# Attention of layer 1: who copies the turned weights out of PSUM

## What is computed

```python
s_loc = jnp.einsum('bnqgrd,bnkgd->bngrqk', qb, kband) * scale      # band of 3 blocks of 128
s_ctx = jnp.einsum('bnqgrd,bkgd->bngrqk', qb, ck) * scale          # 128 cached keys
s_loc = jnp.where(valid, s_loc, MASK_VALUE)
m = jnp.maximum(jnp.max(s, -1), sink)                              # s = both parts in one row
e = jnp.exp(s - m)
p = e / (jnp.sum(e, -1) + jnp.exp(sink - m))
o = p[..., :nk] @ vband + p[..., nk:] @ cv
```

## Time and profile before

| | us |
|---|---|
| median of 3 runs | 2339.85 |
| lowest, highest run | 2335.29, 2341.19 |
| the profiled execution, its own time | 2339.42 |
| its span, first to last instruction | 2337.6 |
| TensorE busy | 2101.0 (90%) |
| VectorE, ScalarE, GpSimd busy | 1437.2, 1266.3, 751.5 |
| mean granted TensorE clock | 0.957 |

### The profile page before, as it was taken

The page is one execution under the profiler, slowest core; times in us unless marked ns, Lnnn a source line. Parts: engine busy times, 40 slices in busy tenths (PEclk is TensorE's granted clock), DMA queues, the critical chain, the costliest instruction groups (busy, mean ns, idle before and its releaser), DMA issues.

```text
span 2337.6 us, 53990 instructions
## 1 busy us (share of the span) xinstructions
PE 2101.0 (90%) x22874; PEld 1285.3 (55%) x22874; DVE 1437.2 (61%) x1779; ACT 1266.3 (54%) x1651; POOL 751.5 (32%) x546
## 2 busy tenths in 40 slices
PE   4999787978989999999899879878879999999994
PEld 3666456845565555555667557645544444444441
DVE  3362656668362121215558667585379999999975
ACT  3534554556444242424543765465378777777762
POOL 0332115433404242424223236432123333333332
PEclk9999898989999999999999989989979999999997
DMA  9442690020312222224231000100367788991124
GB/s 290 138 145 94 217 289 30 4 59 4 93 37 92 71 90 72 86 75 143 90 119 39 1 11 4 45 18 23 131 230 226 240 272 280 321 344 54 32 91 166
DMA packets 246503, 278.45 MB, mean 119 GB/s; under 512 B 61345, under 2 KB 221965, under 8 KB 246159
## 3 DMA queue, kind: packets, MB, share of 16 engines
q1 hardware_dynamic: 237056, 251.99, 34.4%
q0 software_dynamic: 6128, 21.50, 2.5%
q10 hardware_dynamic: 3103, 1.85, 0.3%
HBM read 359.97 MB, written 29.11 MB: 166 GB/s over the span
## 4 chain that ended last, share of the span: by engine, by line
PE 75%; DVE 9%; ACT 8%; issue 3%; DMA 2%; POOL 1%; SPq 1%; DVEq 0%; ACTq 0%; POOLq 0%
PE ps L2307 74%; DVE arena L1674 1%; ACT mix L1460 1%; DVE arena L1678 1%; DVE mix L1674 1%; DMA wbuf<-in_w_mod 1%; DVE small L1902 1%; SPq L726 1%; PE ps L3074 1%; ACT arena L1170 1%; DVE hT L1674 1%; ACT hT L1466 1%; POOL extra L915 1%; ACT arena L1051 1%; DVE const L1674 1%
## 5 line engine op out<-in xcount | busy, mean ns | idle before, releaser
L2307 PE MATMUL ps<-hT,mix 128*128 128x512 f16 (+2 forms) x3024 | 378.1, 287 | 22.7 <-DVE hT L1674 10.4
L2307 PE MATMUL ps<-w,xgT 128*128 128x512 f16 x1632 | 365.6, 381 | 3.6 <-ACT xgT L1571 3.6
L2307 PEld LDWEIGHTS ps<-hT,mix 128*128 128x128 f16 x3024 | 227.4, 99 | 171.1 <-issue 20.7
L2220 DVE SCALAR_TENSOR_TENSOR w<-wst,w 128x2048 f16<-128x2048 f32 x136 | 312.2, 2334 | 5.9 <-ACT w L1557 5.9
L1035 POOL TENSOR_TENSOR a<-aval,a 128x256 f16<-128x256 f32 x68 | 163.3, 2401 | 366.2 <-ACT a L1593 366.2
L2307 PEld LDWEIGHTS ps<-w,xgT 128*128 128x128 f16 x1632 | 157.4, 98 | 182.5 <-ACT xgT L1571 3.9
L1557 ACT ACTIVATE w<-wst 128x2048 f16<-128x2048 f32 x136 | 251.6, 1899 | 3.1 <-DMA xs_rows<-htok,slot_i 3.0
L2307 PE MATMUL ps<-mix 128*128 128x512 f16 (+5 forms) x1856 | 203.3, 287 | 6.2 <-ACT mix L1251 5.7
L2307 PE MATMUL ps<-hT,arena 128*128 128x128 f16 (+1 forms) x1440 | 199.4, 299 | 0.0
L2307 PE MATMUL ps<-w2m,aT 128*128 128x512 f16 x816 | 190.6, 384 | 5.5 <-DVE aT L2247 5.5
L2226 DVE SCALAR_TENSOR_TENSOR w2m<-wst,w2m 128x2048 f16<-128x2048 f32 x68 | 156.0, 2294 | 26.0 <-ACT w2m L1565 25.5
(11 more groups left out here) (354 smaller groups left out, 3464.5 us busy)
## 6 DMA issues: line engine op xcount, KB each, us to landing
wst<-in_moe_w SPq DMA_DIRECT2D x204, 1024.0 KB
wbuf<-in_w_mod SPq DMA_DIRECT2D x40, 1024.0 KB
wbuf<-in_ffn_w SPq DMA_DIRECT2D x33, 1024.0 KB
wbuf<-in_w_in SPq DMA_DIRECT2D x20, 1024.0 KB
xs_rows<-in_table SPq DMA_DIRECT2D x17, 512.0 KB, 6.3
ys_rows<-yb POOLq DMA_DIRECT2D x17, 512.0 KB, 3.2
wbuf<-in_w_out SPq DMA_DIRECT2D x32, 256.0 KB
mix<-in_w_mod SPq DMA_DIRECT2D x1, 4096.0 KB
```

The costliest lines, as they stand in the source:

```text
L2220: v_.scalar_tensor_tensor(out=q[1], in0=staged(s, p), scalar=WS, in1=q[0], op0=ALU.mult, op1=ALU.subtract).then_inc(sg["m_lo13"], 1)
L2307: return mm_(o, w, x, start=first, stop=last, skip_group_check=True)
```

## The change

In layer 1 alone, ScalarE copies only the half of f = 0 of a unit's turned weights. VectorE copies the half of f = 1, in a new function `half(x)`, between `scores(x + 2)` and `divide(x + 1)`. Its copy waits for T of unit x, and from unit 2 on for the product of unit x-2 (which read the buffer that it overwrites). Each copy increments a new semaphore, `t_half`. TensorE waits for it in each unit after `output(x - 1)` and ahead of `side(x)`. PSUM's slot is still given back by ScalarE's copy alone. Layer 0 keeps its one copy.

```diff
-                    copy(a_pT[x % 2][:, :, 0:w], L.full(j).rearrange("p (f w) -> p f w", f=2)[:, :, 0:w], j)
+                    halves_ = 1 if l else 2
+                    copy(a_pT[x % 2][:, 0:halves_, 0:w],
+                         L.full(j).rearrange("p (f w) -> p f w", f=2)[:, 0:halves_, 0:w], j)
...
+                def half(x):
+                    n, t = units[x]
+                    w = window(n)[2]
+                    s = L.full(J(f"T{n}_{t}")).rearrange("p (f w) -> p f w", f=2)
+                    if x >= 2:
+                        L.full(J("O%d_%d" % units[x - 2]))
+                    L.do(v_.tensor_copy(a_pT[x % 2][:, 1, 0:w], s[:, 1, 0:w]), "t_half")
+
                 scores(0)
                 scores(1)
                 divide(0)
                 for x in range(len(units)):
                     if x + 2 < len(units):
                         scores(x + 2)
+                    if l:
+                        half(x)
                     if x + 1 < len(units):
                         divide(x + 1)
...
                     if x:
                         output(x - 1)
+                    if l:
+                        L.need("t_half")
                     side(x)
```

More of the change, by code:

```diff
@@ L519, in backbone_kernel @@
             "pad_cols lb_in lb_exp h_ready pad_zero conv_done conv_silu rope_ready sm_in sm_exp prob_ready "
-            "f_in f_ln lf_ready l2_sq l2_r l2_ready ab_in ab_exp la_ready "
+            "t_half f_in f_ln lf_ready l2_sq l2_r l2_ready ab_in ab_exp la_ready "
             "eg_ready dm_in dm_exp kg_ready egl_ready kd_ready qg_ready cs_ready t_ready t_turned lt_ready "
```

## The result

| | before | changed |
|---|---|---|
| median of 8 runs each, on the same chip, us | 2342.73 | 2350.49 |
| lowest, highest run | 2335.29, 2347.24 | 2346.51, 2357.88 |
| the profiled execution, its own time | 2339.42 | 2346.66 |
| its span | 2337.6 | 2344.8 |
| VectorE, ScalarE busy | 1437.2, 1266.3 | 1452.7, 1259.0 |

The account below looks back on a forecast made before the run. ScalarE was taken to bound units 5 to 8, with no engine full in the 81 us stage. The turns' terms summed to +3.8 us on the profiled 2339.42, forecasting 2343.2 us, range 2337.5 to 2349, no measurable change expected.

Parts of the forecast that it names:

- The prices of the copies: VectorE's copies of 512, 384 and 128 columns at 0.68, 0.56, 0.30 us; ScalarE's halves at 0.60, 0.49, 0.28.
- The loop in units 5 to 9: Copy, side job, scores of x+3, maxima, next copy: 5.47 us a turn against 4.91, four turns, +2.2.
- Unit 4 to 5: Turn without a TensorE side job: scores, maxima and copy take 4.19 us against 3.80, +0.4.
- rival 2: TensorE's clock falls in new gaps of the l2 turns (units 5 to 9): +5.1, 2348.3 us; chance 0.16.
- Units 0 to 3: Two ScalarE logarithms of 2.35 us each in unit 1 hold everything and take in the early copies, +0.1.
- rival 1: ScalarE stays the bound and is relieved in units 5 to 15: -3.8, 2335.6 us; chance 0.12.
- Units 9 to 11: First VectorE's loop, 4.60 us, then the new loop with a kv job, 4.15: 8.75 against 8.12, +0.6.
- Units 11 to 15: To unit 13, 4.03 us a turn against 3.96, +0.1; to unit 15 ScalarE partly decides, counted 0.
- The last units: 128-key units 15 to 19: VectorE becomes the loop, 2.43 us a turn, 9.7 against about 9.3, +0.4.
- Rival 4: The change does nothing, since the added waits end in overlooked slack: 2339.4 us; chance 0.08.
- Rival 3: A pause behind VectorE's added copy, up to its own length (0.68), in ten turns: +6.8 more, 2350.0 us; chance 0.02.

Follow-up runs that it names:

- wait_only: Changed kernel, but ScalarE copies both halves and a small 128x2 VectorE instruction, for which TensorE still waits, replaces VectorE's copy; 2349.33 us, ratio 1.0022.
- scores_first: Changed kernel with TensorE in layer 1 issuing the scores of unit x+3 ahead of its wait and the side job; 2348.19 us, ratio 1.0011.
- first5: The change in units 0 to 4 only, the other units as in the kernel before; 2346.78 us, ratio 1.0013.
- from1: The change in units 1 to 19 only, unit 0 as in the kernel before; 2352.2 us beside 2343.1, one run each.
- work_only: Changed kernel, but ScalarE copies both halves, TensorE has no new wait, and VectorE instead reduces as many columns of another tile; 2344.84 us, ratio 1.0001.
- the repeat: The changed kernel once more, unaltered; 2351.30 us, ratio 1.0027 to the kernel before.
- copy_first: Changed kernel with VectorE's copy placed ahead of scores(x + 2); 2367.77 us, ratio 1.0095.

## Why the prediction came out as it did

- **The prices of the copies: right.** 0.692, 0.557 and 0.292 for 0.68, 0.56 and 0.30 on VectorE; 0.60 on ScalarE. Choosing the float32 row of the same width was what made it so.
- **The loop in units 5 to 9: right, its total helped by luck.** 22.05 against 19.65 is +2.4 for a forecast of +2.2. Two of the turns are 5.46 and 5.45 for 5.47, with TensorE waiting 0.8 for 0.7. The first two, 5.22 and 5.92, are not this loop; one lies below its 5.47, the other above. wait_only (4.93) and scores_first (4.88) take the loop apart by its own terms. The cost was the order: what VectorE waits for is queued on TensorE behind what waits for VectorE.
- **Unit 4 to 5: the step that failed.** The forecast was 4.19 and +0.4; it took 7.26, +3.5. I added up the loop from the maxima on, as if the maxima of unit 6 could start when their scores were ready. But VectorE was in the side addition of unit 3 (2.84 us), and only then came the maxima and the copy. In the kernel before this lateness reached only the division and the exponentials. With the new wait it reaches TensorE, which sits idle for 3.2 us. That is 1.8 us (first5), and 1.7 more goes with the clock. The forecast had no fall of the clock in this turn, neither in its sum nor in rival 2. The clock did not only fall here, though: before, it had fallen in the turn ahead (0.65 in turn 3-4), where the changed kernel kept 1.00 and was 1.07 shorter. Over turns 3 to 5 together the loss is 2.4.
- **Units 0 to 3: "two logarithms hold everything", +0.1: wrong in its reason, nearly right in its sum.** Turn 0-1 lost 1.33 beside GpSimd's squares, and units 1 to 4 won back 1.7. They don't depend on each other: from1 keeps the second (13.67) without the first. The gain has two parts. 0.65 is the shorter copy, 0.33 and 0.32 in the turns 1-2 and 2-3, where ScalarE is the bound, as rival 1 would have it; the other 1.07 is the clock that stayed up in turn 3-4. That the three terms nearly cancel is luck.
- **Units 9 to 11: +0.9 for +0.6**, and it is VectorE's work (work_only has all of it). **Units 11 to 15: -0.1 for +0.1.** Both within what such sums can do.
- **The last units: +0.4 was mis-sized.** It came to +1.5 (+1.1 in the repeat). The forecast counted 2.43 for each turn from unit 15 to 19; they took 2.29, 3.68, 2.64 and 2.30 (before 2.37, 2.78, 2.59, 1.55). The turn from unit 16 to 17 holds the gates, which the sum left out; it came to 3.01 in the repeat. The last turn, 2.30 for 1.55, recurs in every kernel with the change there (2.29 to 2.55). The forecast's 9.3 for before does not follow from the two rows that it names, 1372.93 to 1381; the trace has 9.29 from the copy of unit 15 to that of unit 19. TensorE waits for divisions and copies again and again, and the granted clock is low, 0.66 as the row below shows, where it was 0.82 in 1371 to 1381 before. What share of the loss is the clock's is not shown: over first5's last 10.2 us (1376.60 to 1386.80) it was 0.71, and this part took 10.52 as before. The changed kernel by stretch:

```profile
1375.00:1386.50 11.50, 8.23 (x57) 4.84 (x54) 7.36 (x31) 6.09 (x25) 2.91 (x9) 0.66 0.00 1
```

- **Sum.** +0.1, +0.4, +2.2, +0.6, +0.1, +0.4 became -0.4, +3.5, +2.4, +0.9, -0.1, +1.5: 7.8 for 3.8.
- **Rival 1, ScalarE relieved: did not happen** in the l2 turns. In the changed kernel it shows in the turns 1-2, 2-3 and 14-15, by 0.3 each. All four kv turns show it only in kernels that also have the scores ahead of the wait on TensorE (13.8 for 15.2 us), as the rule of the Trainium skill (TensorEngine Tiling (Array Packing), PSUM Bottleneck) would have it. In these traces, sharing the emptying of PSUM paid in full only where the scores were not queued behind the wait for the second copy and VectorE had room.
- **Rival 2, the clock: right in kind, wrong in place.** It had a chance of 0.16, was put into the l2 turns and priced at +5.1. There the clock was 1.00 at 84% busy (18.59 of 22.05). It fell in unit 4 and at the end, where I had counted none. The price of a turn at the lower clock was the right size: 1.1 to 2.4 forecast, 1.7 (2.3 in the repeat) in turn 4-5.
- **Rival 4, nothing: no**, though the smallness of the effect, 0.37%, is not far from it. **Rival 3, a pause behind the copy: no.** The next instruction starts 0.03 us behind it (1340.44 + 0.69 to 1341.16).

## What to carry to other kernels

Before work is moved to an engine with room, list what is queued behind the new wait on the waiting engine, and ask of each whether the engine that does the moved work waits for it. If so, a loop is closed, and the wait goes behind these or the work ahead of them. Go through the loop turn by turn with the irregular side work in it: here one long side instruction ahead of the moved work cost 3.5 us, the clock included, against 2.4 for four regular turns. And where the receiving engine's own sum of work is within a per cent of the bound, there is nothing to win even then.

## What the hardware did that I had not expected

- **A wait of TensorE can cost more than itself.** Behind gaps of 3.22 and 3.21 us the granted clock was 0.66 in the five microseconds from 1323 and 0.50 in those from 1325, and the way from the gap's end to the next copy of T took 3.83 and 4.43 us; behind 2.75 us the clock stayed at 1.00 and it took 2.63. So 1.2 and 1.8 us were lost on top of the gap. Before, it had also fallen without any such gap, at 1318 to 1323. What exactly decides it was not found.
- **The same turn at three clocks.** With TensorE busy all through, turn 3-4 took 3.77, 4.84 and 5.93 us at granted clocks of 1.00, 0.65 and 0.50, whatever copied its weights.
- **A small VectorE instruction can take seven times its time beside GpSimd:** 1.09 for 0.16 us with two columns, while the added copy from PSUM at the same place kept its 0.56 (1301.53 in the changed kernel). The Trainium skill (SBUF — State Buffer, SBUF: two separate sides) says that the two engines share a pair of ports that one of them holds for a whole instruction; the trace agrees, since the slowed instructions of wait_only end at 1301.13 and 1302.47, within 0.04 us of the ends of two squares that start at 1299.85 and take 1.32 each. The multiplications of 384 columns also took 2.44 for two there and 0.88 for two at 1308.73, before.

Open are the reason for the scatter of several microseconds behind the stage, and the scatter of the turn from unit 16 to 17, 2.67 to 3.92 us over the kernels other than copy_first.
